# RWKV output projection: 512 prompt tokens in one bank and 32 sample tokens in another, in place of two halves of 272

## What is computed

```python
for i in range(DEPTH):                       # 4 layers: HGRN2, attention, RWKV-7, HGRN2
    h = rms_norm(x, W['norm_mix'][i])
    ...                                      # mixer of the layer
    x = x + mixed
    x = x + swiglu(rms_norm(x, W['norm_ffn'][i]), W['ffn_w_in'][i], W['ffn_w_out'][i])
```

```python
o = o + jnp.sum(r * k * r_k, axis=-1, keepdims=True) * v
o = o.reshape(B, T, D_MODEL)
return (o * g) @ w_o, S, h[:, -1]            # w_o is 1024 x 1024
```

## Time and profile before

| | |
|---|---|
| median of the runs | 3316.53 us (3316.15 to 3316.9) |
| span of the profiled execution | 3317.4 us |
| PE busy | 3199.1 us, 96% |
| PEld busy | 3038.7 us, 92% |
| DVE busy | 1829.5 us, 55% |
| ACT busy | 1080.1 us, 33% |
| products of line 608 in the profile | 11136 + 8448 records |
| the output projection of the RWKV layer | 384 of them, between 2098.7 and 2152.6 us |

### The profile page before, as it was taken

One profiled execution on the slowest core, in us unless ns is written; L12 is line 12 of the kernel. 1 busy time (PEld: TensorE's weight loads), 2 busy tenths in 40 slices (PEclk: granted clock), 3 DMA queues, 4 the chain that ended last, 5 costly groups with the idle time before them and its releaser, 6 DMA issues.

```text
span 3317.4 us, 82245 instructions
## 1 busy us (share of the span) xinstructions
PE 3199.1 (96%) x35300; PEld 3038.7 (92%) x35300; DVE 1829.5 (55%) x3015; ACT 1080.1 (33%) x1769; POOL 131.7 (4%) x247
## 2 busy tenths in 40 slices
PE   8998999999998999997999999899999999899998
PEld 7997999998887999996988888899999998799998
DVE  6776643445665543436467786544344666754343
ACT  3232321224555321222434343332223222332221
POOL 0000000002231000000000000000000000000000
PEclk9999999999999999999999999899999999999999
DMA  3322232233443232221210000223232222223222
GB/s 125 104 84 65 90 91 87 87 98 113 125 131 95 86 100 77 89 89 62 83 29 19 16 16 15 68 84 100 77 98 80 85 91 89 73 83 99 79 93 74
DMA packets 104599, 269.09 MB, mean 81 GB/s; under 512 B 12802, under 2 KB 45954, under 8 KB 104146
## 3 DMA queue, kind: packets, MB, share of 16 engines
q1 hardware_dynamic: 91346, 228.54, 22.2%
q0 software_dynamic: 13056, 37.64, 3.4%
HBM read 247.60 MB, written 18.52 MB: 80 GB/s over the span
## 4 chain that ended last, share of the span: by engine, by line
PE 88%; DVE 7%; ACT 2%; DVEq 1%; issue 1%; DMA 0%; SPq 0%; ACTq 0%
PE ps L608 71%; PE ps L1059 5%; PE ps L1051 1%; PE ps L689 1%; PE ps L1155 1%; DVE arena_r L1972 1%; PE ps L906 1%; PE ps L747 1%; PE ps L930 1%; PE ps L770 1%; DVE arena L2420 1%; DVE arena L2580 0%; PE ps L1067 0%; PE ps L755 0%; DMA ring<-in_w_mix 0%
## 5 line engine op out<-in xcount | busy, mean ns | idle before, releaser
L608 PE MATMUL ps<-arena_r 128*128 128x272 f32 x11136 | 1492.0, 292 | 57.9 <-DVE arena_r L2426 16.1
L608 PEld LDWEIGHTS ps<-arena_r 128*128 128x128 f32 x11136 | 1424.1, 190 | 102.6 <-issue 54.2
L608 PE MATMUL ps<-hb_r,arena_r 128*128 128x272 f32 x8448 | 1062.6, 288 | 0.4 <-DVE hb_r L1965 0.4
L608 PEld LDWEIGHTS ps<-hb_r,arena_r 128*128 128x128 f32 x8448 | 1060.5, 188 | 1.1 <-DVE hb_r L1965 0.8
L1450 ACT ACTIVATE arena_r<-ring 128x1024 fp32r<-128x1024 f32 (+1 forms) x240 | 275.3, 1147 | 913.2 <-PE ps L608 913.2
L1991 DVE TENSOR_TENSOR arena_r<-ring,arena_r 128x1024 fp32r<-128x1024 f32 (+1 forms) x240 | 319.7, 1332 | 142.8 <-ACT arena_r L1450 142.8
L2037 DVE TENSOR_TENSOR arena<-ps,rstd 128x544 f32<-128x544 f32 x88 | 63.7, 724 | 293.7 <-PE ps L608 293.7
L2058 DVE TENSOR_TENSOR x<-x,ps 128x544 f32<-128x544 f32 x64 | 46.2, 721 | 292.3 <-PE ps L608 292.3
L1432 ACT ACTIVATE arena_r<-ring 128x1024 fp32r<-128x1024 f32 x80 | 84.6, 1057 | 134.1 <-PE ps L608 128.7
L1497 ACT ACTIVATE arena_r<-arena 128x544 f32 (+1 forms) x88 | 58.0, 659 | 196.8 <-DVE arena L2042 196.8
L2032 DVE TENSOR_TENSOR arena<-ps,rstd 128x544 f32<-128x544 f32 x88 | 63.7, 724 | 94.5 <-PE ps L608 94.2
(11 more groups left out here) (409 smaller groups left out, 3065.1 us busy)
## 6 DMA issues: line engine op xcount, KB each, us to landing
ring<-in_w_up SPq DMA_DIRECT2D x176, 512.0 KB, 3.5
ring<-in_w_mix SPq DMA_DIRECT2D x112, 512.0 KB, 3.5
ring<-in_w_down SPq DMA_DIRECT2D x64, 704.0 KB, 4.1
arena<-in_hg_s POOLq DMA_DIRECT2D x16, 512.0 KB, 3.8
out_hg_so<-arena POOLq DMA_DIRECT2D x16, 512.0 KB, 2.9
ring<-in_w_hgout SPq DMA_DIRECT2D x16, 512.0 KB, 3.5
arena<-in_cache_k SPq DMA_DIRECT2D x128, 64.0 KB, 1.9
arena<-in_cache_v POOLq DMA_DIRECT2D x128, 64.0 KB, 2.2
```

The source lines that it names most:

```text
L608: mm = pe.matmul(PS[:, 2 * a + hf, 0:HALF], part[:, ws], rhs[:, o:o + HALF], start=start and n == 0, stop=stop and n == 2)
```

## The change

`block_product_prompt_whole` takes the place of `block_product` in the output projection of the RWKV layer alone. It issues the same number of products (six a chunk, with the same weights in the same order) with the tokens cut in another way: 512 tokens into bank 2a, and 32 tokens into bank 2a + 1. The DVE addition of line 2744 becomes two additions, one over 512 columns and one over 32, and the semaphore is raised by the second. Waits, weights, buffers and the order of the work stay as they are, and so do all other callers of `block_product`.

```diff
+            def block_product_prompt_whole(a, w, c, hi, lo, start, stop):
+
+                ws = slice(c * P, (c + 1) * P)
+                for n, (part, rhs) in enumerate(((wh3[w], hi), (wh3[w], lo), (wl3[w], hi))):
+                    for bank, t0, t1 in ((2 * a, 0, NP_TOK), (2 * a + 1, NP_TOK, NT)):
+                        mm = pe.matmul(PS[:, bank, 0:t1 - t0], part[:, ws], rhs[:, c * NT + t0:c * NT + t1],
+                                       start=start and n == 0, stop=stop and n == 2)
+                return mm
+
...
-                    mm = block_product((0, 3, 1, 2)[m % 4], m % 2, c, hh, hl, c == 0, c == KC - 1)
+                    mm = block_product_prompt_whole((0, 3, 1, 2)[m % 4], m % 2, c, hh, hl, c == 0, c == KC - 1)
...
-                    xm = halves(X[:, m * NT:(m + 1) * NT])
-                    dve.tensor_tensor(xm, xm, acc((0, 3, 1, 2)[m % 4]), ALU.add).then_inc(S("rw_x"), 1)
+                    a = (0, 3, 1, 2)[m % 4]
+                    xp, xs = X[:, m * NT:m * NT + NP_TOK], X[:, m * NT + NP_TOK:(m + 1) * NT]
+                    dve.tensor_tensor(xp, xp, PS[:, 2 * a, 0:NP_TOK], ALU.add)
+                    dve.tensor_tensor(xs, xs, PS[:, 2 * a + 1, 0:NS_TOK], ALU.add).then_inc(S("rw_x"), 1)
```

## The result

The changed kernel takes 3387.04 us (median of two runs, 3386.39 to 3387.69) against 3316.53 us: +70.5 us, a ratio of 1.0207 with a 95% interval of 1.0188 to 1.0225. The forecast was 3332.5 us, in a range that ended at 3354.

The account below looks back on a forecast made before the run. PE's products of line 608 were taken to bound the output projection. 183 pairs on the path at +87.7 ns each gave +16.0 us on 3316.5, so 3332.5 us, with a range from 3328 to 3354 us.

Parts of the forecast that it names:

- The path: Output projection: 78 + 288 = 366 products, or 183 pairs sharing a chunk and part, lie on the chain; +16.0 us.
- the other nine: Output projection pairs off the path, six before the wait on DVE, three beside ACT and DVE; without cover +0.8 us.
- the small product's price: The 32-column product costs the weight load that follows it: 113 ns, bounds 110 and 125.
- rival A: Output projection: the load is hidden after all, a pair stays 250.6 ns, 3316.5 us; chance 0.07.
- B: Rival: fp32r weights load faster when pressed, about 295 ns a pair, +8.2 us, 3324.7 us; chance 0.04.
- C: Rival: a 32-column product takes two passes and two loads, 449 ns a pair, +36.4 us, 3352.9 us; chance 0.15.
- the two waits of PE in the stage: Waits on DVE's low part and on lines 1860 and 2643: 2.7 and 1.5 us in place of 3.25 and 1.75.
- the three covered pairs: Chunk 7 of m = 1: 1.01 in place of 0.75 us, covered by 2.33 us of ACT and DVE.
- The large product: The 512-column product: 213.3 ns of streaming plus 12.0 ns, 225.3 ns; 216 to 235.9 ns between the bounds.
- 12.0 ns: Today's cost of a 272-column product beyond its columns' 113.3 ns; taken as a cost per product.
- rival D: The clock falls to 1.2 GHz for the stage: 552 ns a pair, +55 us; chance 0.03, 0.02 of that beyond 2%.
- point of decision: Rival D decides at +66 us, 2%, reached if the low clock lasts another 100 products of the feed-forward.

Follow-up runs that it names:

- The three cuts: Pairs of 416 + 128, 464 + 80 and 512 + 32 columns at the upper clock, in changed forms of the kernel before: 300.0, 322.3 and 344.4 ns.
- Both filled: Changed kernel plus 24 useless products in PE's first idle stretch and 12 ahead of m = 2: 3335.85 us, ratio 1.0044 to the kernel before.
- 512 + 128: Changed kernel with the second product streaming 128 columns, only the last 32 used: 3332.98 us, ratio 1.0047 to the kernel before.
- the run with DVE's part alone: Kernel before, PE's products kept in halves of 272 columns, only DVE's addition split in two: 3320.29 us, ratio 1.0004.
- 496 + 48: Changed kernel with the 544 columns of a pair cut as 496 and 48: 3387.72 us, ratio 1.0209 to the kernel before.
- the run again: The changed kernel unaltered, five more executions: 3382.89 us, ratio 1.0199 to the kernel before.
- one filling: Changed kernel plus 24 useless 272-column products in PE's first idle stretch: median 3351.54 us, ratio 1.0102 to the kernel before.
- 416 + 128: Changed kernel with the 544 columns of a pair cut as 416 and 128: 3326.66 us, ratio 1.0026 to the kernel before.
- 464 + 80: Changed kernel with the 544 columns of a pair cut as 464 and 80: 3334.27 us, ratio 1.0047 to the kernel before.
- the reordered products: Changed kernel with each m's 24 large products before its 24 small ones in m = 2 to 7: 3350.61 us, ratio 1.0103 to the kernel before.

## Why the prediction was wrong

**What held.** The path: 183 pairs, in a chain of the same two pieces, and the other nine under cover. The load as the small product's price, 108 ns: it is not hidden (rival A) and not faster for this type (B). One pass (C): 384 records. DVE: 680 and 180 ns for my 692 and 180, and no cost. Of the two waits of PE in the stage, the first is 2.9 us (2.7 forecast); the second is 0.6 where I said 1.5, because the three covered pairs run at half clock.

**The size of the pair at the upper clock.** I said 225.3 + 113 = 338.3 ns; measured are 344.4. The large product was the mis-sized term. I had to choose whether today's 12.0 ns above 272 columns at one a cycle are a cost of each product or grow with the columns, and took the first. The three cuts show the second, 0.46 ns a column (125.3 / 272 is 0.461), so 235.9 ns, my upper bound. The small one is 108 for my 113. The sum at the upper clock becomes 183 × 93.8 ns = +17.2 us for my +16.0. Both filled gave +16.0 and 512 + 128 gave +17.2.

**The step that failed** is the clock under the pair. The sum takes all 183 pairs at a granted clock of 1.00, and gives rival D, "the clock falls", a chance of 0.03. The runs showed 0.50 from about 2100 to 2219 and 640 ns a pair in place of 338.3. Nearly all of the miss is there: 70.4 − 17.2 = 53 us, against 1.2 us from the size of the pair. D's two reasons "against" were both weak, each in its own way:

- "PE never idles in the stage for longer than today." True, and no protection. The idle stretch of today already takes the clock in the kernel with halves (the run with DVE's part alone). The question was not what takes it but what gives it back, and I did not ask it.
- "That stretch, with products far shorter than these, was still granted 0.91." That was a mean over 26 us. Behind it stand 12 us at 0.50, and the stage starts from there. The mean of 1.00 over the stage likewise says how the clock stood under halves, and nothing of what another form of the work would do.

The prediction worked out the pair at the upper clock in full and never asked what the same pair does once the clock is low: there the load takes 213 ns too, and in the changed kernel the clock did not come back until the halves of the feed-forward.

**The price of D** was short too: 552 ns a pair, measured 640. I halved the streaming (512 / 1.2) and left the load at 113 ns. The pair at half clock is 640 = 427 for 512 columns and 213 for the rest, twice the load's price at the upper clock; 496 + 48 agrees, 626.7 − 413.3 = 213.4. So D reaches its point of decision without the feed-forward: 183 × 389 ns = +71 us, which is the first measured result (the run again gave +63.9), and the feed-forward has the clock back about a microsecond in.

**What remains open.** What exactly takes the clock. The profile of the kernel before keeps it through an idle stretch of 3.25 us, while others lose it in the same place, three profiles (one filling, 416 + 128, 464 + 80) lost it behind a wait of 1.5 to 1.6 us, and the reordered products lost it with PE never idle. Also open is why 512 + 32 and 496 + 48 don't bring it back where wider second products do: the runs show that they don't, and not by what rule. With one filling the executions of one program came out both ways, so it is not in the program alone. Seven of seven executions of the changed kernel lost it.

## What to carry to other kernels

A cut of a product into unequal parts costs the weight load that the small part no longer covers; that can be read from any row with short products, and here it was +17 us as summed. But before trusting such a sum, look at the granted clock in short windows around the stage. Ask what may take it there (waits of PE, runs of short products), and what the new form costs at the lower level, where its loads are slower too, should it not come back. If that is the risk, columns of no use beside the load are a remedy to try: 96 of them cost 1.2 ns a pair here and returned some 50 us. The better choice in this kernel was to leave the halves as they are.

## What the runs showed of the hardware

- One form of work can stand at either level of the granted clock for as long as it lasts: 512 + 32 held 1.00 for 49.6 us in one run (both idle stretches filled) and 0.50 for 118 us in another (the changed kernel). Which one is not fixed by the form; with one filling, executions of one program came out both ways (3334 and 3368 to 3381 us).
- The clock can fall while PE is never idle: with the small products of an m last, it went to 0.50 about a microsecond behind 24 products of 32 columns, and came back some 3 us later under products of 512.
- Weight loads follow the clock: the small product, which costs its load, takes 108 ns at 2.4 GHz and 213 ns at 1.2 GHz. The Trainium skill ("TensorE: Matmul & The Clock Gate", section "LDWEIGHTS (loading the stationary operand)") gives the time of a load in ns as its columns divided by 1.2, without a word on the clock. By that I estimate 107 ns for 128 columns, which agrees with the upper level (108) and is half of what was measured at the lower one (213).
- A product of type fp32r costs 0.46 ns a column from 272 to 512 columns at the upper clock, some 10% over a cycle each, and no fixed part on top that these runs could tell. At the lower clock there is no such surplus: 640.0 − 626.7 = 13.3 ns for 16 columns is 0.83 ns a column, a cycle at 1.2 GHz.
